# One more pair of gate panels by the seven-product scheme: 30 instead of 28 of 32, with token blocks made sooner and PSUM banks mirrored

## Chip, cores and metric

One core of one Trainium2 chip. The metric is the device time of one execution in microseconds (us). Engines are called by their names in the profile: PE (TensorE, matmuls), PEld (its weight loads), DVE (VectorE), ACT (ScalarE), POOL (GpSimd), SP (SyncE, which here only starts transfers). Two times of this kernel that differ by under 0.2% (2.2 us) can't be told from no change.

## What is computed

Two layers, one behind the other, on 512 tokens of width 1024. The change lies in the end of the second:

```
h = rms_norm_2(x, norm_g)
proj = h @ w_in                      # its last 4 x 1024 columns are the gates
...
ys = jnp.stack([y_a, y_b, y_c, y_d], axis=0)           # four branches, 512 wide each
branch_d = jnp.einsum('nbsw,nwd->bsnd', ys, w_branch)
g = jax.nn.sigmoid(gates.reshape(bsz, s, N_BRANCH, d))
merged = jnp.sum(g * branch_d, axis=2)
return x + merged @ w_out
```

followed by a last RMS norm. All products are to fp32 accuracy: every operand is split in two fp32r parts, hi and lo, and each product of two operands is three matmuls (hi hi, hi lo, lo hi).

## The kernel before, in words

The program is written out by hand for each engine, with semaphores between them. The work is a list of **units**, `USED`; PE, ACT and DVE each walk the same list in order, and each engine's own queue is strictly in order. A unit is mostly one weight strip of 128 x 1024. For unit number k:

- SP fetches strips into a ring of five raw buffers, in the order of the list; a buffer is free once the strip in it has been split (`raw_done`, `lo_made`).
- ACT, in its turn for unit k, first makes the hi part of the strip of unit k+3 (`split_hi`, L665, one copy). DVE, in its turn for unit k, first forms a sum or difference of weights for unit k+4 where there is one (`combine`), then makes the lo part of unit k+3 (`split_lo`, L1201, one subtraction). Then both do what unit k's own results want: ACT a sigmoid or copies out of PSUM, DVE products and sums. ACT waits for PE's end of unit k ahead of those (not in units `sa` and `br`).
- PE multiplies the strip with the transposed tokens hT, 8 tiles of 128 x 512, hi and lo.

The gates are 32 panels `ga` of 128 output columns, the branches' output products are 16 units `br`; pair p = 2 panels `ga 2p`, `ga 2p+1` and one unit `br p`. A panel done plainly is 8 tiles x 3 = 24 matmuls of 512 columns (`panel`, `product`, L1896 to L1898). Pairs 2 to 15 are done instead by a seven-product scheme (as Strassen's, in Winograd's form): the two panels, 1024 inputs and 512 tokens are cut in halves, and seven products of quarters are made, each 4 x 3 = 12 matmuls of 256 columns (`quarters`, L1904 to L1908). They are spread over the units `sa` (2 products), `sb` (2), `br` (1, between the two halves of the branch product; the branch product itself is 24 matmuls of 512), `sc` (1) and `sd` (1), in the function `strassen`. Pairs take turns in the PSUM banks side and acc (`banks_of`).

The chain within one pair: after the first product of `sa` (12 matmuls) ACT copies it out of bank 0 to gate_a (semaphore `part_kept`); the second half of unit `sb` adds to that bank and therefore waits for this copy. The copy stands in ACT's turn for unit `sa`, behind `split_hi` of the unit three further on. The product in the middle of `br` waits likewise for a second copy, and for the lo weights of `sc`.

The scheme needs **token blocks** that are sums and differences of quarters of hT: T1, T2, T4 (with hi and lo) and T3, which is written over the quarter (0,1) of hT once no plain panel reads that any more. `make_tokens` (DVE) makes each: three chained 128 x 1024 operations for the full value (`difference`, L1227 to L1229; T3 and T4), one subtraction for the lo part; ACT makes the hi part with a copy. T1 and T2 are made long before, in units `dq` and `dk`. The order around the change, before it (one unit each, plain letters for plain units):

```
dz3 | ga0 | ga1 | br0 | ga2 | ga3 | br1 | sa2 | sb2 | br2 | sc2 | sd2 | sa3 ...
DVE: dz3 -; ga0 four y_d tiles; ga1 T3 full; ga2 T4 full; ga3 T4 lo; br1 T3 lo
ACT: ga0 hi of four y_d tiles; ga3 T4 hi, then T3 hi
```

In DVE's turn for ga0 the last branch, y_d, is ended: four times a product (L1430), a copy by ACT (L918), a subtraction (L1434), in lockstep. For the first pair by the scheme, `sb` wants T1 and T2, the middle product of `br` wants T3 lo, and `sc` wants T4 lo.

Of the kernel before, what the change touches and what calls it, by code (L numbers as in the profile page):

```python
# [6 lines left out]
P = 128  # L7
S = 512
# [42 lines left out]

FIRST_PAIR, LAST_PAIR = 2, 2 * KT - 1
USED = []
for u in ORDER:
    if u[0] == "br" and u[1] >= FIRST_PAIR:
# [180 lines left out]
def program(nc, dram, out):  # L238
    f32, f32r, bf16, i32 = mybir.dt.float32, mybir.dt.float32r, mybir.dt.bfloat16, mybir.dt.int32
    ALU, ACT, AX = mybir.AluOpType, mybir.ActivationFunctionType, mybir.AxisListType  # L240
    with ExitStack() as ctx:
# [159 lines left out]
        t_rest = {n: at(f"t{n}_rest", r, [P, 4, HALF]) for n, r in ((1, R_B), (4, M + 16384))}  # L401
        t_full = {n: at(f"t{n}_full", r + 4096, [P, 4, HALF]) for n, r in ((1, R_B), (2, R_B + 8192), (4, M + 16384))}
        s12 = at("s12", M + 24576, [P, 2, 4 * P])
        t3_part = at("t3_part", M + 24576, [P, 4, HALF])
        t3_full = at("t3_full", M + 28672, [P, 4, HALF])
        gate_a = at("gate_a", R_0, [P, S])
        gate_b = at("gate_b", M + 28672, [P, HALF])
        x2_kept = nc.dram_tensor("x2_kept", (S, D), f32, kind="Internal").ap()
# [98 lines left out]
        def strip_of(k):  # L507

            kind, j = USED[k]
            if kind == "sa":  # L510
                return raw_of(("ga", 2 * j))
            if kind == "sb":
                return s12[:, :, :].rearrange("p a c -> p (a c)")
            if kind == "sc":
                return raw_of(("ga", 2 * j + 1))
            if kind == "sd":
                return raw_of(("ga", 2 * j))[:, 512:1024]
            return raw[:, UNIT[kind, j] % RING, 0:WIDTH.get(kind, U)]

        def banks_of(p):  # L520

            return side if p % 2 == 0 else acc

        def ada_tile(j):
            return ada_raw[j % ADA_RING // 4][:, j % 4, :]
# [116 lines left out]
        def _(act):  # L642
# [238 lines left out]
            for k, (kind, j) in enumerate(USED):  # L881
# [168 lines left out]
                if (kind, j) in (("dq", 2), ("dq", 3)):  # L1050
                    n = j - 1
                    act.wait_ge(t_step, T_STEP[n, "full"])
                    nc.scalar.activation(t_hi[n][:, :, :], t_full[n][:, :, :], ACT.Copy).then_inc(t_hi_made, 1)
                if (kind, j) == ("ga", 3):
                    act.wait_ge(t_step, T_STEP[4, "full"])
                    nc.scalar.activation(t_hi[4][:, :, :], t_full[4][:, :, :], ACT.Copy).then_inc(t_hi_made, 1)
                    act.wait_ge(t_step, T_STEP[3, "full"])
                    nc.scalar.activation(quarter(hT_hi, 0, 1), t3_full[:, :, :], ACT.Copy).then_inc(t_hi_made, 1)
# [50 lines left out]
        def _(dve):  # L1109
# [94 lines left out]
            def combine(k):  # L1204

                kind, j = USED[k] if k < len(USED) else (None, 0)
                if kind not in ("sb", "sc", "sd"):
                    return
                a, b, n = raw_of(("ga", 2 * j)), raw_of(("ga", 2 * j + 1)), j - FIRST_PAIR + 1
                if kind == "sb":  # L1210
                    for u in (("ga", 2 * j), ("ga", 2 * j + 1)):
                        dve.wait_ge(raw_in[UNIT[u] % RING], 16 * (UNIT[u] // RING + 1))
                    then(nc.vector.tensor_tensor(out=s12[:, 0, :], in0=b[:, 0:512], in1=b[:, 512:1024], op=ALU.add))
                    nc.vector.tensor_tensor(out=s12[:, 1, :], in0=s12[:, 0, :], in1=a[:, 0:512], op=ALU.subtract)\
                        .then_inc(combined, 1)
                if kind == "sc":
                    nc.vector.tensor_tensor(out=b[:, 0:512], in0=a[:, 0:512], in1=b[:, 0:512], op=ALU.subtract)\
                        .then_inc(combined, 1)
                if kind == "sd":
                    dve.wait_ge(combined, 3 * (n - 1) + 1)  # L1220
                    dve.wait_ge(lo_made, STEP["sa", j] + 1)
                    nc.vector.tensor_tensor(out=a[:, 512:1024], in0=a[:, 512:1024], in1=s12[:, 1, :], op=ALU.subtract)\
                        .then_inc(combined, 1)

            def difference(dst, part, hi, lo, hi_less, lo_less):
# [5 lines left out]
            def make_tokens(kind, j):  # L1231

                hi = {(r, c): quarter(hT_hi, r, c).bitcast(f32) for r in (0, 1) for c in (0, 1)}
                lo = {(r, c): quarter(hT_lo, r, c).bitcast(f32) for r in (0, 1) for c in (0, 1)}
                full, rest = {n: t[:, :, :] for n, t in t_full.items()}, {n: t[:, :, :] for n, t in t_rest.items()}
                if (kind, j) == ("dq", 1):
                    dve.wait_ge(x2_saved, 16)
                    difference(full[1], rest[1], hi[0, 1], lo[0, 1], hi[0, 0], lo[0, 0])
                if (kind, j) == ("dq", 2):
                    dve.wait_ge(t_step, T_STEP[1, "full"])  # L1240
                    then(nc.vector.tensor_tensor(out=full[2], in0=hi[1, 1], in1=full[1], op=ALU.subtract))
                    nc.vector.tensor_tensor(out=full[2], in0=full[2], in1=lo[1, 1], op=ALU.add).then_inc(t_step, 1)
                if (kind, j) in (("dq", 3), ("dk", 0)):
                    n = 1 if kind == "dq" else 2
                    dve.wait_ge(t_step, T_STEP[2, "full"])
                    dve.wait_ge(t_hi_made, n)
                    nc.vector.tensor_tensor(out=t_lo[n][:, :, :], in0=full[n], in1=t_hi[n][:, :, :].bitcast(f32),
                                            op=ALU.subtract).then_inc(t_step, 1)
                if (kind, j) == ("ga", 1):
                    difference(t3_full[:, :, :], t3_part[:, :, :], hi[1, 1], lo[1, 1], hi[0, 1], lo[0, 1])  # L1250
                if (kind, j) == ("ga", 2):
                    dve.wait_ge(t_step, T_STEP[2, "lo"])
                    difference(full[4], rest[4], hi[1, 0], lo[1, 0],
                               t_hi[2][:, :, :].bitcast(f32), t_lo[2][:, :, :].bitcast(f32))
                if (kind, j) == ("ga", 3):
                    dve.wait_ge(t_step, T_STEP[4, "full"])
                    dve.wait_ge(t_hi_made, 3)
                    nc.vector.tensor_tensor(out=t_lo[4][:, :, :], in0=full[4], in1=t_hi[4][:, :, :].bitcast(f32),
                                            op=ALU.subtract).then_inc(t_step, 1)
                if (kind, j) == ("br", 1):  # L1260
                    dve.wait_ge(t_step, T_STEP[3, "full"])
                    dve.wait_ge(t_hi_made, 4)
                    nc.vector.tensor_tensor(out=quarter(hT_lo, 0, 1), in0=t3_full[:, :, :],
                                            in1=quarter(hT_hi, 0, 1).bitcast(f32), op=ALU.subtract).then_inc(t_step, 1)

            def gate_pair(kind, j):
# [12 lines left out]
                if kind == "sd":  # L1279
# [5 lines left out]
                    for o in (1, 0):  # L1285
                        dve.wait_ge(unit_used, STEP["br", j] + 1)
                        dve.wait_ge(sig_made, 3 * p + 3 - o)
                        first = j % 2 == 0 and o == 1
                        nc.vector.tensor_tensor(out=total if first else merged_part[:, :], in0=(acc if o == 0 else side)[3][:, :],
                                                in1=sig[:, o, :], op=ALU.mult).then_inc(gated, 1)  # L1290
                        dve.wait_ge(gated, 2 * p + 2 - o)
                        if not first:
# [285 lines left out]
            for k, (kind, j) in enumerate(USED):  # L1578
# [271 lines left out]
                if (kind, j) == ("w2", 3):  # L1850
                    for t in range(TT):
                        if t == 0:
                            dve.wait_ge(x2_here, 32)
                        wait_tile(dve, (kind, j), t)
                        nc.vector.tensor_tensor(out=x2[t][:, 0:S], in0=side[t][:, :], in1=x2[t][:, 0:S],
                                                op=ALU.add).then_inc(freed["dve"], 1)
                if (kind, j) == ("w2", 4):

# [8 lines left out]
                if (kind, j) == ("w2", 7):  # L1867
# [5 lines left out]

                    for t in range(TT):
                        wait_tile(dve, (kind, j), t)
                        nc.vector.tensor_tensor(out=x2[t][:, S:D], in0=acc[t][:, :], in1=x2[t][:, S:D],
                                                op=ALU.add).then_inc(freed["dve"], 1)
                        if t:
                            finish_right(t - 1)
# [3 lines left out]
        def _(pe):  # L1883
# [28 lines left out]
            def strassen(k, kind, j):  # L1912
# [4 lines left out]
                if kind == "sa":  # L1917
# [3 lines left out]
                        pe.wait_ge(bank2_read, len(BANK2))  # L1921
                        pe.wait_ge(bank3_read, 2 * TT)
                    elif p == 1:
                        wait_freed(pe, RESULT["br", 1] + 1)
                    else:
                        pe.wait_ge(sig_made, 3 * (p - 1))
                    quarters(ps[0], w, 0, h[0, 0]).then_inc(part_made, 1)
# [8 lines left out]
                if kind == "br":  # L1936
                    hi, lo = weights(k)
                    if p == 0:
                        wait_freed(pe, RESULT["br", 1] + 1)
                    else:  # L1940
                        pe.wait_ge(gated, 2 * p)
                    for o in range(2):
                        if o == 1:
# [3 lines left out]
                                pe.wait_ge(t_step, T_STEP[3, "lo"])  # L1947
                            quarters(ps[0], w, 0, h[0, 1], first=False).then_inc(part_made, 1)
                        name = "abcd"[2 * (j % 2) + o]
                        for kt in range(4):  # L1950
                            cols = slice((4 * o + kt) * P, (4 * o + kt + 1) * P)
                            ins = product((acc if o == 0 else side)[3][:, :], (hi[:, cols], lo[:, cols]),
                                          (y_hi[name][:, kt, :], y_lo[name][:, kt, :]), kt == 0, kt == 3)
                    ins.then_inc(unit_used, 1)
                if kind == "sc":
# [24 lines left out]
            def token_units(k, kind, j, source, width, x_ready=None, tile_done=None, early=None):  # L1980

                per, count = TOKEN_UNITS[kind], TOGETHER.get((kind, j), 1)
                for t in range(TT):
# [4 lines left out]
                    for i in range(count - 1, -1, -1):  # L1988
                        hi, lo = weights(k - i, t == 0)
                        first, last = (j - i) % per == 0, (j - i) % per == per - 1  # L1990
                        if kind == "w2":
# [4 lines left out]
                            if (j - i, t) == (4, 0):  # L1996
                                pe.wait_ge(sig_made, 3 * (LAST_PAIR - FIRST_PAIR + 1))
                                pe.wait_ge(gated, 2 * (LAST_PAIR - FIRST_PAIR + 1))
                            ps = (side if j - i < per else acc)[t]
                        else:  # L2000
                            ps = bank(r) if first else acc[r % 4]
                        for a in range(2):
# [486 lines left out]
```

## Time and profile before

| | |
|---|---|
| median of 3 runs | 1106.76 us (1106.72 to 1107.06) |
| the profiled execution | 1106.82 us |
| its span, first to last instruction | 1104.9 us |
| PE busy | 1096.4 us, 99% of the span |
| PEld / DVE / ACT / POOL busy | 84% / 68% / 47% / 2% |
| mean granted clock of PE | 0.998 |
| DMA | 121.09 MB, mean 110 GB/s |

The execution is 1.9 us longer than its span. Busy time of PE counts a matmul to the end of its pipeline, so matmuls that follow one another overlap in it; what a matmul costs is the distance from its start to the next one's start.

### The profile page before, as it was taken

To read this page: it belongs to the slowest core of one execution; us is meant where nothing else is said; L and a number is where in the kernel's file an instruction comes from. 1 tells how busy PE (TensorE), PEld (TensorE's weight loads), DVE (VectorE), ACT (ScalarE), POOL (GpSimd) and SP (SyncE) were. 2 spreads that over 40 slices of the span, in tenths; PEclk is the share of its full clock that TensorE was granted. 3 is DMA by queue.
4 is the path that set the end of the run, shared out by engine and by line. 5 is a ranking of instruction groups with operands and counts; after the bars stand their busy time and mean duration, and the time that the engine had idled before them with its cause. 6 is when DMAs were issued, how large, how long until landed. Compare 5 with 4: busy or idle time off the path is not lost.

```text
span 1104.9 us, 17994 instructions
## 1 busy us (share of the span) xinstructions
PE 1096.4 (99%) x7298; PEld 928.7 (84%) x7298; DVE 748.9 (68%) x1202; ACT 517.5 (47%) x870; POOL 17.8 (2%) x40
## 2 busy tenths in 40 slices
PE   9999999999999999999999999999999999999997
PEld 8888888888888888878888887887789999999986
DVE  6876876954676247458789887447568777667853
ACT  7662354324675235544453535336544444444543
POOL 1000000000001001000000000000000000000000
PEclk9999999999999999999999999999999999999999
DMA  9543324422214422622222232231121322333241
GB/s 371 221 152 125 120 74 133 125 98 78 77 58 144 161 90 104 200 66 86 79 77 96 77 96 77 63 109 58 58 77 58 115 100 73 115 114 115 83 185 77
DMA packets 33618, 121.09 MB, mean 110 GB/s; under 512 B 3824, under 2 KB 3824, under 8 KB 33536
## 3 DMA queue, kind: packets, MB, share of 16 engines
q1 hardware_dynamic: 30672, 109.88, 29.2%
q0 software_dynamic: 2720, 10.03, 2.6%
q8 instruction: 58, 0.95, 0.3%
q14 instruction: 24, 0.20, 0.1%
q10 hardware_dynamic: 144, 0.03, 0.0%
HBM read 115.74 MB, written 4.19 MB: 109 GB/s over the span
## 4 chain that ended last, share of the span: by engine, by line
PE 98%; DMA 1%; ACT 0%; SPq 0%; DVE 0%; issue 0%
PE acc L1896 22%; PE acc L1898 22%; PE acc L1897 22%; PE acc L1908 2%; PE side L1908 2%; PE acc L1906 2%; PE side L1906 2%; PE acc L1904 2%; PE side L1904 2%; PE side L1896 2%; PE side L1897 2%; PE side L1898 2%; PE acc L2271 2%; PE side L2051 2%; PE side L2271 1%; PE side L2123 1%
## 5 line engine op out<-in xcount | busy, mean ns | idle before, releaser
L1201 DVE TENSOR_TENSOR w_lo<-raw,w_hi 128x1024 fp32r<-128x1024 f32 (+2 forms) x194 | 225.7, 1165 | 148.9 <-ACT w_hi L665 146.1
L1896 PE MATMUL acc<-hT_hi,w_hi 128*128 128x512 f32 x648 | 258.6, 399 | 0.0
L1898 PE MATMUL acc<-hT_hi,w_lo 128*128 128x512 f32 x648 | 252.8, 390 | 0.0
L1897 PE MATMUL acc<-hT_lo,w_hi 128*128 128x512 f32 x648 | 252.4, 389 | 0.0
L665 ACT ACTIVATE w_hi<-raw 128x1024 fp32r<-128x1024 f32 (+2 forms) x194 | 195.4, 1008 | 109.8 <-PE acc L1898 82.4
L1896 PEld LDWEIGHTS acc<-hT_hi,w_hi 128*128 128x128 f32 x648 | 121.8, 188 | 27.1 <-issue 2.4
L1898 PEld LDWEIGHTS acc<-hT_hi,w_lo 128*128 128x128 f32 x648 | 121.6, 188 | 26.0
L1897 PEld LDWEIGHTS acc<-hT_lo,w_hi 128*128 128x128 f32 x648 | 121.9, 188 | 23.6
L1896 PE MATMUL acc<-w_hi,hT_hi 128*128 128x512 f32 (+1 forms) x152 | 59.9, 394 | 0.0
L1898 PE MATMUL acc<-w_hi,hT_lo 128*128 128x512 f32 (+1 forms) x152 | 58.8, 387 | 0.0
L1897 PE MATMUL acc<-w_lo,hT_hi 128*128 128x512 f32 (+1 forms) x152 | 58.7, 386 | 0.0
L1201 DVE TENSOR_TENSOR w_lo<-s,w_hi 128x1024 fp32r<-128x1024 f32 x14 | 17.1, 1225 | 39.7 <-ACT w_hi L665 39.7
L944 ACT ACTIVATE silu_e<-acc 128x512 f32<-128x512 f32 x32 | 18.9, 592 | 53.6 <-PE acc L1898 53.6
L1896 PEld LDWEIGHTS acc<-w_hi,hT_hi 128*128 128x128 f32 x152 | 28.5, 188 | 6.1 <-issue 0.8
L1898 PEld LDWEIGHTS acc<-w_hi,hT_lo 128*128 128x128 f32 x152 | 28.5, 188 | 5.6
L1897 PEld LDWEIGHTS acc<-w_lo,hT_hi 128*128 128x128 f32 x152 | 28.6, 188 | 5.2
L1908 PE MATMUL side<-hT_hi,w_lo 128*128 128x256 f32 x112 | 31.7, 283 | 0.0
L1908 PE MATMUL acc<-hT_hi,w_lo 128*128 128x256 f32 x112 | 31.7, 283 | 0.0
L1906 PE MATMUL side<-hT_lo,w_hi 128*128 128x256 f32 x112 | 31.7, 283 | 0.0
L1906 PE MATMUL acc<-hT_lo,w_hi 128*128 128x256 f32 x112 | 31.7, 283 | 0.0
L1904 PE MATMUL acc<-hT_hi,w_hi 128*128 128x256 f32 x112 | 31.7, 283 | 0.0
L1904 PE MATMUL side<-hT_hi,w_hi 128*128 128x256 f32 x112 | 31.7, 283 | 0.0
(482 smaller groups left out, 2249.0 us busy)
## 6 DMA issues: line engine op xcount, KB each, us to landing
raw<-in_ga SPq DMA_DIRECT2D x32, 512.0 KB, 4.8
ada_raw<-in_ada SPq DMA_DIRECT2D x16, 512.0 KB, 11.5
raw<-in_wo SPq DMA_DIRECT2D x16, 512.0 KB, 3.5
raw<-in_br SPq DMA_DIRECT2D x16, 512.0 KB, 3.5
raw<-in_q SPq DMA_DIRECT2D x8, 512.0 KB, 3.5
raw<-in_u SPq DMA_DIRECT2D x8, 512.0 KB, 3.9
raw<-in_gp SPq DMA_DIRECT2D x8, 512.0 KB, 4.8
raw<-in_ada_w SPq DMA_DIRECT2D x8, 512.0 KB, 3.5
```

Of the source, the lines that this page charges most:

```text
L665: nc.scalar.activation(split_at(k)[0][:, 0:WIDTH.get(kind, U)], strip_of(k), ACT.Copy).then_inc(hi_made, 1)
L944: nc.scalar.activation(gate_e(gates), acc[RESULT[kind, j] % 4][:, :], ACT.Exp, scale=-1.0)\
L1201: nc.vector.tensor_tensor(out=lo[:, 0:width], in0=strip_of(k), in1=hi[:, 0:width].bitcast(f32), op=ALU.subtract).then_inc(lo_made, 1)
L1896: nc.tensor.matmul(ps, w[0], x[0], start=first, stop=False)
L1897: nc.tensor.matmul(ps, w[0], x[1], start=False, stop=False)
L1898: return nc.tensor.matmul(ps, w[1], x[0], start=False, stop=last)
L1904: nc.tensor.matmul(out_, w[0][:, cols], x[0][:, kt, :], start=first and kt == 0, stop=False, skip_group_check=not first)
L1906: nc.tensor.matmul(out_, w[0][:, cols], x[1][:, kt, :], start=False, stop=False, skip_group_check=not first)
L1908: ins = nc.tensor.matmul(out_, w[1][:, cols], x[0][:, kt, :], start=False, stop=kt == 3, skip_group_check=not first)
L2051: ins = nc.tensor.matmul(ps[p0:p0 + B, n0:n0 + width], k[:, tok], right, start=True, stop=True)
L2123: ins = nc.tensor.transpose(side[2][:, b * P:(b + 1) * P], probs[:, s % 2, b * P:(b + 1) * P], ident[:, :])
L2271: return nc.tensor.matmul((acc + side)[h][:, :], w[:, h * P:(h + 1) * P], x[:, j, :], start=start and j == 0, stop=stop and j == KT - 1)
```

## The change

Pair 1 (panels ga2 and ga3) goes by the seven-product scheme too. `FIRST_PAIR` becomes 1, and the list reads `dz3 | ga0 | ga1 | br0 | sa1 | sb1 | br1 | sc1 | sd1 | sa2 ...`. DVE makes T3 full in its turn for dz3 (was ga1), T4 full for ga1 (was ga2), T4 lo for br0 (was ga3), T3 lo for sa1 (was br1). ACT makes T4 hi and T3 hi in its turn for br0 (was ga3). The sum of weights of the first pair has a place of its own (`s12_first`), as has T3. Banks: the first pair still begins in side, so all later pairs, and the two halves of the last product, change sides.

```diff
-FIRST_PAIR, LAST_PAIR = 2, 2 * KT - 1
+FIRST_PAIR, LAST_PAIR = 1, 2 * KT - 1
...
+        s12_first = at("s12_first", M + 4096, [P, 2, 4 * P])
-        t3_part = at("t3_part", M + 24576, [P, 4, HALF])
-        t3_full = at("t3_full", M + 28672, [P, 4, HALF])
+        t3_part = at("t3_part", M + 8192, [P, 4, HALF])
+        t3_full = at("t3_full", M + 12288, [P, 4, HALF])
...
-        def banks_of(p):
+        def s12_of(j):
+            return s12_first if j == FIRST_PAIR else s12
+        def banks_of(j):
-            return side if p % 2 == 0 else acc
+            return side if (j - FIRST_PAIR) % 2 == 0 else acc
...
-                if (kind, j) == ("ga", 3):
+                if (kind, j) == ("br", 0):
+                    act.wait_ge(unit_used, STEP["ga", 1] + 1)
                     act.wait_ge(t_step, T_STEP[4, "full"])
                     nc.scalar.activation(t_hi[4][:, :, :], t_full[4][:, :, :], ACT.Copy).then_inc(t_hi_made, 1)
                     act.wait_ge(t_step, T_STEP[3, "full"])
...
+                if (kind, j) == ("dz", 3):
+                    difference(t3_full[:, :, :], t3_part[:, :, :], hi[1, 1], lo[1, 1], hi[0, 1], lo[0, 1])
                 if (kind, j) == ("ga", 1):
-                    difference(t3_full[:, :, :], t3_part[:, :, :], hi[1, 1], lo[1, 1], hi[0, 1], lo[0, 1])
-                if (kind, j) == ("ga", 2):
                     dve.wait_ge(t_step, T_STEP[2, "lo"])
                     difference(full[4], rest[4], hi[1, 0], lo[1, 0],
                                t_hi[2][:, :, :].bitcast(f32), t_lo[2][:, :, :].bitcast(f32))
-                if (kind, j) == ("ga", 3):
+                if (kind, j) == ("br", 0):
...
-                if (kind, j) == ("br", 1):
+                if (kind, j) == ("sa", 1):
                     dve.wait_ge(t_step, T_STEP[3, "full"])
...
-                        wait_freed(pe, RESULT["br", 1] + 1)
+                        wait_freed(pe, RESULT["br", 0] + 1)
...
+                        if p == 0:
+                            pe.wait_ge(y_made, 1 + FINAL.index((name, 3)))
                         for kt in range(4):
                             cols = slice((4 * o + kt) * P, (4 * o + kt + 1) * P)
-                            ins = product((acc if o == 0 else side)[3][:, :], (hi[:, cols], lo[:, cols]),
+                            ins = product((side if o == 0 else acc)[3][:, :], (hi[:, cols], lo[:, cols]),
...
-                            ps = (side if j - i < per else acc)[t]
+                            ps = (acc if j - i < per else side)[t]
```

The reads of these banks by DVE (branch products times gates, and the two sums with the residual at the end) change sides with them.

## Rows read from the trace of the kernel before

**Rows 1.** The page's part 1 and the chain of waits (part 4), share of the span.

```profile
PE 1096.4 (99%) x7298; PEld 928.7 (84%) x7298; DVE 748.9 (68%) x1202; ACT 517.5 (47%) x870; POOL 17.8 (2%) x40
...
PE 98%; DMA 1%; ACT 0%; SPq 0%; DVE 0%; issue 0%
```

**Rows 2.** PE's timeline, 821 to 853 us: start, length, line, out<-in.

```profile
821.04 0.39 PE L1896 MATMUL acc<-hT_hi,w_hi 128*128 128x512 f32 x1
...
837.36 0.28 PE L1904 MATMUL side<-hT_hi,w_hi 128*128 128x256 f32 x1
...
843.11 0.40 PE L1896 MATMUL acc<-ya_hi,w_hi 128*128 128x512 f32 x1
...
845.86 0.28 PE L1904 MATMUL side<-hT_hi,w_hi 128*128 128x256 f32 x1
...
847.29 0.40 PE L1896 MATMUL side<-yb_hi,w_hi 128*128 128x512 f32 x1
...
850.04 0.28 PE L1904 MATMUL side<-t_hi,w_hi 128*128 128x256 f32 x1
...
852.91 0.28 PE L1904 MATMUL acc<-hT_hi,w_hi 128*128 128x256 f32 x1
```

**Rows 3.** DVE's timeline, 803 to 843 us; in brackets idle time before, releaser.

```profile
803.75 0.43 DVE L1372 TENSOR_SCALAR silu_e<-silu_e 128x512 f32<-128x512 f32 x1 [2.65 <-ACT silu_e L944]
806.48 1.22 DVE L1201 TENSOR_TENSOR w_lo<-raw,w_hi 128x1024 fp32r<-128x1024 f32 x1 [2.31 <-ACT w_hi L665]
...
808.27 0.68 DVE L1430 TENSOR_TENSOR y_tmp<-z_d,yd_raw 128x512 f32<-128x512 f32 x1
...
819.07 1.23 DVE L1201 TENSOR_TENSOR w_lo<-raw,w_hi 128x1024 fp32r<-128x1024 f32 x1 [2.10 <-ACT w_hi L665]
820.22 1.22 DVE L1227 TENSOR_TENSOR t_full<-hT_hi 128x1024 f32<-128x1024 f32 x1
...
822.73 1.23 DVE L1229 TENSOR_TENSOR t_full<-t_full,t_part 128x1024 f32<-128x1024 f32 x1
823.87 1.22 DVE L1201 TENSOR_TENSOR w_lo<-raw,w_hi 128x1024 fp32r<-128x1024 f32 x1
825.01 0.68 DVE L1831 TENSOR_TENSOR m_full<-acc,sig 128x512 f32<-128x512 f32 x1
...
827.17 0.69 DVE L1213 TENSOR_TENSOR s<-raw 128x512 f32<-128x512 f32 x1
...
828.51 1.22 DVE L1201 TENSOR_TENSOR w_lo<-raw,w_hi 128x1024 fp32r<-128x1024 f32 x1
...
841.48 0.68 DVE L1222 TENSOR_TENSOR raw<-raw,s 128x512 f32<-128x512 f32 x1
842.08 1.22 DVE L1201 TENSOR_TENSOR w_lo<-raw,w_hi 128x1024 fp32r<-128x1024 f32 x1
```

**Rows 4.** ACT's timeline, 833 to 839 us.

```profile
833.42 1.06 ACT L1056 ACTIVATE t_hi<-t_full 128x1024 fp32r<-128x1024 f32 x1 [0.70 <-DVE t_full L1229]
834.38 1.04 ACT L1058 ACTIVATE hT_hi<-t_full 128x1024 fp32r<-128x1024 f32 x1
835.33 1.04 ACT L665 ACTIVATE w_hi<-raw 128x1024 fp32r<-128x1024 f32 x1
...
838.99 0.38 ACT L1064 ACTIVATE gate_a<-side 128x256 f32<-128x256 f32 x1
```

**Rows 5.** SP's timeline and the transfers of 780 to 860 us, median landing time last.

```profile
807.73 0.33 SPq L564 DMA_DIRECT2D raw<-in_br  x1
...
raw<-in_br SPq DMA_DIRECT2D x3, 512.0 KB, 3.7
```

**Rows 6.** The last matmul, then stretches: length, busy PE, ..., granted clock (PEclk), DMA.

```profile
1098.52 0.39 PE L1898 MATMUL acc<-w_hi,m_lo 128*128 128x512 f32 x1
...
1101.00:1102.00 1.00, 0.00 (x0) 0.00 (x0) 0.75 (x1) 0.72 (x1) 0.00 (x0) 0.76 0.80 328
1102.00:1103.00 1.00, 0.00 (x0) 0.00 (x0) 0.00 (x0) 0.00 (x0) 0.00 (x0) 0.50 0.87 344
```

More of the change, by code:

```diff
@@ L512, in strip_of @@
             if kind == "sb":
-                return s12[:, :, :].rearrange("p a c -> p (a c)")
+                return s12_of(j)[:, :, :].rearrange("p a c -> p (a c)")
             if kind == "sc":
@@ L1208, in combine @@
                     return
+                part = s12_of(j)
                 a, b, n = raw_of(("ga", 2 * j)), raw_of(("ga", 2 * j + 1)), j - FIRST_PAIR + 1
@@ L1212, in combine @@
                         dve.wait_ge(raw_in[UNIT[u] % RING], 16 * (UNIT[u] // RING + 1))
-                    then(nc.vector.tensor_tensor(out=s12[:, 0, :], in0=b[:, 0:512], in1=b[:, 512:1024], op=ALU.add))
-                    nc.vector.tensor_tensor(out=s12[:, 1, :], in0=s12[:, 0, :], in1=a[:, 0:512], op=ALU.subtract)\
+                    then(nc.vector.tensor_tensor(out=part[:, 0, :], in0=b[:, 0:512], in1=b[:, 512:1024], op=ALU.add))
+                    nc.vector.tensor_tensor(out=part[:, 1, :], in0=part[:, 0, :], in1=a[:, 0:512], op=ALU.subtract)\
                         .then_inc(combined, 1)
@@ L1221, in combine @@
                     dve.wait_ge(lo_made, STEP["sa", j] + 1)
-                    nc.vector.tensor_tensor(out=a[:, 512:1024], in0=a[:, 512:1024], in1=s12[:, 1, :], op=ALU.subtract)\
+                    nc.vector.tensor_tensor(out=a[:, 512:1024], in0=a[:, 512:1024], in1=part[:, 1, :], op=ALU.subtract)\
                         .then_inc(combined, 1)
@@ L1288, in gate_pair @@
                         first = j % 2 == 0 and o == 1
-                        nc.vector.tensor_tensor(out=total if first else merged_part[:, :], in0=(acc if o == 0 else side)[3][:, :],
+                        nc.vector.tensor_tensor(out=total if first else merged_part[:, :], in0=(side if o == 0 else acc)[3][:, :],
                                                 in1=sig[:, o, :], op=ALU.mult).then_inc(gated, 1)
@@ L1854, in _ @@
                         wait_tile(dve, (kind, j), t)
-                        nc.vector.tensor_tensor(out=x2[t][:, 0:S], in0=side[t][:, :], in1=x2[t][:, 0:S],
+                        nc.vector.tensor_tensor(out=x2[t][:, 0:S], in0=acc[t][:, :], in1=x2[t][:, 0:S],
                                                 op=ALU.add).then_inc(freed["dve"], 1)
@@ L1875, in _ @@
                         wait_tile(dve, (kind, j), t)
-                        nc.vector.tensor_tensor(out=x2[t][:, S:D], in0=acc[t][:, :], in1=x2[t][:, S:D],
+                        nc.vector.tensor_tensor(out=x2[t][:, S:D], in0=side[t][:, :], in1=x2[t][:, S:D],
                                                 op=ALU.add).then_inc(freed["dve"], 1)
@@ L1938, in strassen @@
                     if p == 0:
-                        wait_freed(pe, RESULT["br", 1] + 1)
+                        wait_freed(pe, RESULT["br", 0] + 1)
                     else:
```

## Prediction

> **What bounds the kernel now.** First the page: PE is busy 99% of the span, and 98% of the chain of waits is PE's [rows 1]. So a saving on PE counts in full, and so does every wait put on PE; the other engines have room on the whole (DVE 68%), which says nothing of a single stretch. So I read the timelines of PE, DVE and ACT around the change, 795 to 855 us. On PE, units follow one another without a gap, also from plain panels into the first pair by the scheme [rows 2]. On DVE there is idle time before 819 us (2.3 us before the subtraction at 806.48, 2.1 us before that at 819.07), and from there on none: operation follows operation until past 842 [rows 3]. The token blocks are made there. That stretch decides.
>
> **PE's work.** Plainly, pair 1 takes 821.04 to 837.36 = 16.32 us (72 matmuls of 512 columns, 0.2267 us each). By the scheme, pair 2 takes 837.36 to 852.91 = 15.55 us [rows 2]. 48 matmuls of 512 become 84 of 256, 0.1198 us each (48 of them from 837.36 to 843.11). The columns fall by an eighth, the time by less, since half the columns take more than half of 0.2267. **Gain: 0.77 us.**
> By the Trainium skill (TensorE: Matmul & The Clock Gate, "Back-to-back issue gap") a matmul costs its columns at 2.4 GHz and 2.5 ns; that would make 48 x 215.8 - 84 x 109.2 ns = 1.2 us, an estimate; the trace has 227 and 120 ns for this mix with weight loads, so the trace's 0.77 us stands.
> Even without any new wait the gain is thus 0.07%, a third of what can be told from no change (0.2%, 2.2 us).
>
> **DVE in the new order.** Start to start [rows 3]: a full token block 3.65 us (820.22 to 823.87); a 1024 subtraction 1.15 (819.07 to 820.22); both weight sums of `sb` 1.34 (827.17 to 828.51); one weight difference 0.60 (841.48 to 842.08); gating br0 2.16 (825.01 to 827.17).
> - dz3: T3 can start behind the bound of the gate at 803.75, so at 804.1, and ends DVE's work there at 807.75. Before, DVE was idle until 806.48.
> - ga0: weight sums of `sb1`, new here, 1.34: 809.1. Then w_lo and gate as before (1.79, 806.48 to 808.27): 810.9 instead of 808.27. **DVE is 2.6 us late.** The four y_d tiles are in lockstep with ACT, and ACT's first sigmoid and next weight copy come behind them, so this isn't won back: the subtraction of 819.07 comes at 821.7. It is now `sb1`'s strip, done 822.9; PE wants it at 823.9: in time, with 1 us to spare.
> - ga1: T4 full runs where T3 full ran, 2.6 us later: 822.8, last of three operations at 825.3, ended **826.6**.
> - br0: from 826.5 (1.15 after T4's last start) difference for `sc1` 0.6, w_lo of `br1` 1.15 (ended 828.3), gating 2.16, T4 lo 1.15 (ended 831.7): 831.6.
> - sa1: difference for `sd1` 0.6, w_lo of `sc1` 1.15 (ended 833.4), then T3 lo, 1.22 long, 833.35 to **834.6**.
>
> **ACT in the new order** [rows 4]. In its turn for br0 it now waits for T4 full, and queued behind that wait are T4 hi, T3 hi, the hi weights of `sc1`, and, in the turn for sa1, the copy to gate_a for which PE waits. Before, T3 hi ended at 835.4 and the copy came at 838.99, when PE's first product was there: the wait for T4 was over before `sa2` began, since br1 lay between. Now: T4 hi 826.6, T3 hi 827.6, w_hi 828.5 (0.95 each), copy 829.5 to **829.85**.
>
> **PE in the new order** [rows 2]. br0 still ends at 821.04. `sa1` 24 x 0.12 = 2.9: 823.9. First half of `sb1` 1.44: 825.35. Then the wait for the copy, to 829.9: **4.5 us of idle PE, the first new wait.** Second half of `sb1` to 831.35; first half of the branch product 2.75 (843.11 to 845.86): 834.1; w_lo of `sc1` is ready since 833.4, T3 lo isn't: to 834.6, **0.5 us, the second.** What is left of the pair is 852.91 - 845.86 = 7.05 us: `sa2` starts at 841.65 instead of 837.36. **+4.3 us** = 4.5 + 0.5 - 0.77. T4 lo (831.7) and y_d (819.6) are in time. From `sa2` on the order and the relative times are those of today's pairs, which have no wait, and PE never has slack in which to win it back.
>
> **Beside it, at nothing.** SP: the raw buffer of ga2 is free only after `sd1` (w_lo about 835.4) instead of at 807.7, and `br2`'s strip and those of the next panels queue behind that. It lands some 3.7 us later [rows 5], 839.1; ACT wants it after `sc1` ends, about 840.3. If that cover were gone, each us of lateness would be one on PE; bounds 0 and +1, I take 0. The weight sums of `sb1` want both strips of pair 1 in ga0; they follow dz2 and dz3 in the ring and are there tens of us before. POOL's transfers wait for the same named units. Mirrored banks and halves move no work and no time. New waits of PE for branches c and d repeat semaphores long reached. DVE's four operations that gate br1 are four in the new way too; the three short sums of products that come with a pair (gate_a, gate_b) lie behind T3 lo, where today's pairs leave DVE idle time.
>
> **PE's clock.** After the last matmul ended (1098.9), the granted clock read 1.00, then 0.76 over 1101 to 1102 and 0.50 after [rows 6]: it fell to 1.2 GHz at about 1101.5, after 2.6 us of idle PE. The new gap is 4.4 us, so it can fall here. No row has a matmul at the lower level; at it, a spacing doubles. Bounds: 0 if it doesn't fall; if it stays low for all of the 4.2 us of work up to the wait for T3 lo, +4.2, less the 0.5 that this wait gives back: +3.7. I take a short fall, as likely as none: low for about as long as it took to fall, 2.6 us, costs 1.3 - 0.5 = 0.8, half of which is **+0.4**.
> The Trainium skill (same page, "Why this matters for your kernels") warns that a pause of this kind between bursts puts the clock back to half; by it the clock falls for certain, and the rival below gains.
>
> **Sum**: 1106.82 (the profiled execution: span 1104.9 and 1.9 around it; 0.06 over the median of 1106.76) - 0.77 + 4.55 + 0.5 + 0.4 = **1111.5 us**.
>
> **Rivals.**
> - The clock falls and stays low up to the next wait. For: [rows 6]. Against: at the start of that work PE is fully busy again. Time 1111.1 + 1.2 to 3.7 = 1112.3 to 1114.8. Chance 0.20.
> - Not slower: T3 in dz3 costs DVE nothing. For: 2.3 us were idle before the subtraction at 806.48 and 2.1 us at 819.07. Were DVE not late at all, T4 full would end at 824.0, the copy at 827.3: a wait of 1.9, then 0.5 for T3 lo, less 0.77: 1108.5, within 0.2%. It decides once DVE is less than 0.5 us late at 819. Against: T3 and the weight sums are 5.0 us and only 2.3 of idle time precede, while the 2.1 us at 819 are a wait for ACT, which is shifted as well. Chance 0.06.
> - No new wait on PE at all, if the copy to gate_a doesn't stand behind T4's wait in ACT's queue as I read the list: 1106.05, gain alone. The order in the code speaks against it. Chance 0.05, of which 0.01 for a gain of over 0.2% by something not seen here.
> - The ring: `br2`'s strip and its followers are late on top of the two waits. For: it is fetched 28 us later than now; three transfers start together. Against: today's pairs live with the same distance. 1 us more, 1112.5. Chance 0.06.
> - The forecast, 1110.6 to 1112.3: chance 0.63.
>
> **Numbers.** Faster by over 0.2% 0.02; within 0.2% (1104.6 to 1109.0) 0.11; slower 0.87. The range leaves out the two cases below 1109 and the top of the clock's: 1109.6 to 1113.6.
>
> **What would show it.** PE's timeline: no gap between the first two units of the scheme, then a gap of about 4.5 us in the middle of `sb1` put down to ACT's gate_a, a shorter one in the middle of `br1` put down to DVE's hT_lo; PE idle by some 5 us more, the number of matmuls up by 36. ACT: T4 hi at about 826.6, with 4 to 5 us of idle time before it, released by DVE's T4 full. DVE: the first y_d product at 810.9. Granted clock around 829 to 834: 1.00, or 0.50 in part. Wrong would be: `sb1` without a gap (the ACT order is misread), DVE on time at 819 (T3 was free), a later gap before `br2` (the ring).

## The result, and the profile after

The changed kernel took 1112.11 us in the median of 5 runs (1111.85 to 1113.21), the kernel before 1106.76 us: **0.52% slower** (ratio 1.0052, 95% interval 1.0041 to 1.0062), 5.35 us. Five more runs, beside another series of 21 runs of the kernel before, gave 1113.05 against 1106.97 us (1.0053, 1.0041 to 1.0066). The profiled execution shown here is the longest of the first five, 1113.21 us, 6.4 us over that of the kernel before.

The page of the changed kernel (span; part 1; the chain of part 4):

```profile
span 1111.3 us, 18091 instructions
...
PE 1098.6 (99%) x7334; PEld 932.3 (84%) x7334; DVE 754.3 (68%) x1211; ACT 520.0 (47%) x876; POOL 17.8 (2%) x40
...
PE 96%; DVE 1%; ACT 1%; DMA 1%; issue 0%; SPq 0%; DVEq 0%; ACTq 0%
```

PE has 36 matmuls more, and its share of the chain fell from 98% [rows 1] to 96%; DVE and ACT, at 0% before, now have 1% each. PE's timeline (start, length, line, out<-in, in brackets idle time before and its releaser; answers to [rows 2]):

```profile
820.83 0.28 PE L1910 MATMUL side<-hT_hi,w_hi 128*128 128x256 f32 x1
...
825.02 0.28 PE L1914 MATMUL side<-t_hi,w_lo 128*128 128x256 f32 x1
829.64 0.58 PE L1910 MATMUL side<-t_hi,w_hi 128*128 128x256 f32 x1 [4.34 <-ACT gate_a L1069]
830.02 0.41 PE L1912 MATMUL side<-t_lo,w_hi 128*128 128x256 f32 x1
...
832.37 0.63 PE L1902 MATMUL side<-yc_hi,w_hi 128*128 128x512 f32 x1
832.80 0.63 PE L1903 MATMUL side<-yc_lo,w_hi 128*128 128x512 f32 x1
...
836.02 0.39 PE L1902 MATMUL side<-yc_hi,w_hi 128*128 128x512 f32 x1
836.25 0.39 PE L1903 MATMUL side<-yc_lo,w_hi 128*128 128x512 f32 x1
...
836.72 0.28 PE L1910 MATMUL side<-hT_hi,w_hi 128*128 128x256 f32 x1
...
843.76 0.28 PE L1910 MATMUL acc<-hT_hi,w_hi 128*128 128x256 f32 x1
```

br0 ends and `sa1` begins at 820.83, 0.21 us earlier than in the execution of before. The first half of `sb1` issues its last matmul at 825.02; then PE is idle for 4.34 us and is released by ACT's copy to gate_a. What follows is to be read by its spacing, the distance from one matmul's start to the next one's: 829.64 to 832.37 is 12 matmuls in 2.73 us, 0.21 us each once the first is through (0.12 before), and 832.37 to 832.80 is 0.43 us for a matmul of 512 columns (0.227 before). Not until 836.02 is the spacing 0.23 again. `sa2` begins at 843.76: 22.93 us after `sa1`, where the pair has 15.55 us of work. By spacing, the 7.38 us between them are the wait (825.14 to 829.64, 4.50) and the slow stretch behind it (829.64 to 836.72 is 7.08 us for work that takes 4.19, 1.44 + 2.75, in the rows of before).

DVE's timeline (answers to [rows 3]: T3's first operation, first y_d product, w_lo of `sb1`, T4's last operation, T3 lo):

```profile
803.88 1.22 DVE L1233 TENSOR_TENSOR t_full<-hT_hi 128x1024 f32<-128x1024 f32 x1
...
810.60 0.68 DVE L1436 TENSOR_TENSOR y_tmp<-z_d,yd_raw 128x512 f32<-128x512 f32 x1
...
821.40 1.23 DVE L1206 TENSOR_TENSOR w_lo<-s_first,w_hi 128x1024 fp32r<-128x1024 f32 x1 [2.10 <-ACT w_hi L669]
...
825.05 1.23 DVE L1235 TENSOR_TENSOR t_full<-t_full,t_rest 128x1024 f32<-128x1024 f32 x1
...
832.98 1.22 DVE L1269 TENSOR_TENSOR hT_lo<-t_full,hT_hi 128x1024 fp32r<-128x1024 f32 x1
```

ACT's timeline (answers to [rows 4]: T4 hi, T3 hi, w_hi of `sc1`, the copy to gate_a):

```profile
826.37 1.06 ACT L1061 ACTIVATE t_hi<-t_full 128x1024 fp32r<-128x1024 f32 x1 [3.57 <-DVE t_full L1235]
827.34 1.04 ACT L1063 ACTIVATE hT_hi<-t_full 128x1024 fp32r<-128x1024 f32 x1
828.28 1.04 ACT L669 ACTIVATE w_hi<-raw 128x1024 fp32r<-128x1024 f32 x1
829.23 0.36 ACT L1069 ACTIVATE gate_a<-side 128x256 f32<-128x256 f32 x1
```

The y_d tiles start 2.33 us later than at 808.27 [rows 3] (2.54 if the 0.21 us between the executions are counted), T4 full ends at 826.28, and behind it ACT makes four copies back to back. The last of them, the copy of 0.36 us to gate_a, is what PE wants; it ends at 829.59.

PE's granted clock in stretches of one us (length, busy PE, PEld, DVE, ACT, POOL, clock, DMA share, GB/s; answers to [rows 6]):

```profile
828.00:829.00 1.00, 0.00 (x0) 0.00 (x0) 0.96 (x3) 1.00 (x2) 0.00 (x0) 0.98 0.00 0
829.00:830.00 1.00, 0.35 (x1) 0.36 (x2) 0.97 (x2) 0.59 (x2) 0.00 (x0) 0.50 0.00 0
...
834.00:835.00 1.00, 1.00 (x4) 0.73 (x3) 1.00 (x3) 0.00 (x0) 0.00 (x0) 0.50 0.00 0
835.00:836.00 1.00, 1.00 (x4) 0.79 (x3) 0.97 (x3) 0.00 (x0) 0.00 (x0) 0.61 0.02 8
836.00:837.00 1.00, 1.00 (x7) 0.84 (x6) 1.00 (x2) 0.00 (x0) 0.00 (x0) 1.00 0.56 184
```

The clock fell at 828.96 (0.98 over the us from 828), 3.7 us after PE's last matmul had ended, and stayed at its lower level of 1.2 GHz for 6.8 us, to 835.8 (a reading of 0.61 over one us means 0.78 us at the lower level). The strip of `br2` is fetched where it was forecast, and PE never waits for it:

```profile
835.16 0.33 SPq L568 DMA_DIRECT2D raw<-in_br  x1
```

### The profile page after: what moved, and what is told of

It is laid out like the page before. It is cut to its first block, busy times and chain, and to the rows that moved or that the text cites. A ratio compares the mean times of both kernels' runs of the same rounds, so it can differ in the third digit from the quotient of the medians.

```text
span 1111.3 us, 18091 instructions
## 1 busy us (share of the span) xinstructions
PE 1098.6 (99%) x7334; PEld 932.3 (84%) x7334; DVE 754.3 (68%) x1211; ACT 520.0 (47%) x876; POOL 17.8 (2%) x40
## 3 DMA queue, kind: packets, MB, share of 16 engines
HBM read 115.74 MB, written 4.19 MB: 108 GB/s over the span
## 4 chain that ended last, share of the span: by engine, by line
PE 96%; DVE 1%; ACT 1%; DMA 1%; issue 0%; SPq 0%; DVEq 0%; ACTq 0%
PE acc L1902 21%; PE acc L1904 21%; PE acc L1903 21%; PE side L1910 2%; PE side L1914 2%; PE side L1912 2%; PE side L1902 2%; PE side L1903 2%; PE side L1904 2%; PE acc L1914 2%; PE acc L1912 2%; PE acc L1910 2%; PE acc L2279 2%; PE side L2059 2%; PE side L2279 1%; PE side L2131 1%
## 5 line engine op out<-in xcount | busy, mean ns | idle before, releaser
L1902 PE MATMUL acc<-hT_hi,w_hi 128*128 128x512 f32 x632 | 252.4, 399 | 0.0
L1904 PE MATMUL acc<-hT_hi,w_lo 128*128 128x512 f32 x632 | 246.5, 390 | 0.0
L1903 PE MATMUL acc<-hT_lo,w_hi 128*128 128x512 f32 x632 | 246.1, 389 | 0.0
L1902 PEld LDWEIGHTS acc<-hT_hi,w_hi 128*128 128x128 f32 x632 | 118.8, 188 | 26.5 <-issue 2.4
L1904 PEld LDWEIGHTS acc<-hT_hi,w_lo 128*128 128x128 f32 x632 | 118.6, 188 | 25.4
L1903 PEld LDWEIGHTS acc<-hT_lo,w_hi 128*128 128x128 f32 x632 | 118.9, 188 | 23.0
L1914 PE MATMUL side<-hT_hi,w_lo 128*128 128x256 f32 x128 | 36.2, 283 | 0.0
L1912 PE MATMUL side<-hT_lo,w_hi 128*128 128x256 f32 x128 | 36.2, 283 | 0.0
L1910 PE MATMUL side<-hT_hi,w_hi 128*128 128x256 f32 x128 | 36.2, 283 | 0.0
L1910 PE MATMUL side<-t_hi,w_hi 128*128 128x256 f32 x96 | 27.8, 290 | 4.3 <-ACT gate_a L1069 4.3
```

The source lines that it names most:

```text
L1902: nc.tensor.matmul(ps, w[0], x[0], start=first, stop=False)
L1903: nc.tensor.matmul(ps, w[0], x[1], start=False, stop=False)
L1904: return nc.tensor.matmul(ps, w[1], x[0], start=False, stop=last)
L1910: nc.tensor.matmul(out_, w[0][:, cols], x[0][:, kt, :], start=first and kt == 0, stop=False, skip_group_check=not first)
L1912: nc.tensor.matmul(out_, w[0][:, cols], x[1][:, kt, :], start=False, stop=False, skip_group_check=not first)
L1914: ins = nc.tensor.matmul(out_, w[1][:, cols], x[0][:, kt, :], start=False, stop=kt == 3, skip_group_check=not first)
```

## Experiments

All runs of a group share their runs of the kernel before: 1106.78 us (1106.59 to 1107.05) for the first four, 1106.97 us (1106.81 to 1107.53) for the last three, another chip with 0.19 us more. That 0.19 us is taken off where the two groups are compared. Most differences between these kernels are under the 0.2% that can't be told from no change by one comparison; what is said of them rests on series of runs that don't overlap, and on the waits in the traces.

### Is ACT's order at fault, or DVE's chain?

```diff
-                if (kind, j) == ("br", 0):
-                    act.wait_ge(unit_used, STEP["ga", 1] + 1)
-                    act.wait_ge(t_step, T_STEP[4, "full"])
-                    nc.scalar.activation(t_hi[4][:, :, :], t_full[4][:, :, :], ACT.Copy).then_inc(t_hi_made, 1)
...
                     nc.scalar.activation(gate_a[:, 0:HALF], banks_of(j)[0][:, 0:HALF], ACT.Copy).then_inc(part_kept, 1)
+                    if p == 0:
+                        act.wait_ge(t_step, T_STEP[4, "full"])
+                        nc.scalar.activation(t_hi[4][:, :, :], t_full[4][:, :, :], ACT.Copy).then_inc(t_hi_made, 1)
...
```

> ACT's copies T4 hi and T3 hi moved from its turn for br0 to its turn for sa1, behind the copy to gate_a. Theory (DVE's chain sets the time, ACT's queue only passes it on): the hi weights of sc1 still stand ahead of the copy and want DVE's weight difference, ended 826.9; so the copy ends about 828.3 and the first gap of PE shrinks from 4.5 to about 3.1 us, but T3 lo comes at 834.2 as before and PE waits there for 1.7 us more if its clock is high. Time 1110.9 with the clock at 1.00, about 1112.1 if it falls as in the changed kernel: within 0.3 us of 1111.1 or of 1112.1, no gain to speak of. Rival (ACT's order alone is at fault): the gap's 1.4 us are gained in full, 1110.7 or less beside 1112.1, and no second gap.

Measured: 1111.14 us (1111.10 to 1111.26), 1.0039 (1.0027 to 1.0052). PE's two gaps, from its timeline:

```profile
828.47 0.39 PE L1909 MATMUL side<-t_hi,w_hi 128*128 128x256 f32 x1 [3.00 <-ACT gate_a L1063]
...
834.52 0.36 PE L1909 MATMUL side<-hT_hi,w_hi 128*128 128x256 f32 x1 [1.60 <-DVE hT_lo L1268]
```

The first gap shrank by 1.34 us to 3.00, and a second of 1.60 us opened, for T3 lo. The clock reads 1.00 all through the units of pair 1 in this execution, and by spacing the two waits are 3.16 and 1.76 us: together 4.9, as in the forecast for the changed kernel (4.5 + 0.5). (One of the five runs had a mean clock of 0.997 and was no longer than the others; a second wait of this length can take a slow stretch up, which is argued, not shown. So the times of this kernel don't tell whether the clock fell.) The theory holds: a better order on ACT only moves the wait to the next thing that DVE's chain makes late. Beside the changed kernel it is 1 us faster all the same, and the next run tells what that us was.

### What is the clock's part?

```diff
+                    if p == 0:
+                        wait_freed(pe, RESULT["ga", 1])
+                        for _ in range(36):
+                            nc.tensor.matmul(acc[RESULT["ga", 1] % 4][:, 0:HALF], w[0][:, 0:P],
+                                             t[1][0][:, 0, :], start=True, stop=True)
                     pe.wait_ge(part_kept, 3 * p + 1)
```

> 36 more matmuls of 256 columns (4.3 us at 0.12 us each) put on PE in the middle of sb1, ahead of its wait for the copy to gate_a, into an accumulator bank that is free then; their result is not used. Theory (the low clock after the gap is worth the difference between the wait alone and what was measured): granted clock 1.00 all through 825 to 840 us, spacings of 0.12 and 0.227 us behind the gap, T3 lo awaited for 0.5 us, time 1111.0 to 1111.2 in every run, 1 us under the changed kernel's median and with a spread of 0.2 us instead of 1.4. Rival (the clock has no part in it, the spread comes from elsewhere): 1112.1 and the same spread; or slower, if these matmuls disturb DVE's reads.

Measured: 1111.17 us (1110.98 to 1111.41). Clock in stretches of 2 us:

```profile
828.00:830.00 2.00, 1.97 (x17) 1.77 (x16) 1.93 (x4) 1.79 (x3) 0.00 (x0) 1.00 0.00 0
830.00:832.00 2.00, 2.00 (x15) 1.91 (x16) 1.97 (x3) 0.00 (x0) 0.00 (x0) 1.00 0.03 8
...
834.00:836.00 2.00, 1.75 (x14) 1.50 (x13) 1.97 (x5) 0.01 (x1) 0.00 (x0) 1.00 0.01 4
```

PE does 4.3 us of work for nothing, and the kernel is 0.94 us faster by the medians. The clock stays at 1.00, T3 lo is awaited (0.25 us of idle PE, 0.40 by spacing), and the time is the forecast's without its clock term, 1111.1. The spread is 0.4 us instead of 1.4, twice the 0.2 expected, with two of the five runs (1111.33 and 1111.41) above the 1111.2 that was expected at the most. So the rest of what the changed kernel lost is the clock.

The changed kernel once more, in the second group:

> The changed kernel as it is, for more runs of it beside the others. Theory (a gap of 4.3 us, and the clock falls behind it in every run, at a moment that differs): all runs above the 1111.2 of the kernel with the filled gap, from 1111.8 to 1113.3, the more the lower the mean clock. Rival (it falls in some runs only): some runs at 1111.0 to 1111.3.

Measured: 1113.05, 1113.35, 1112.32, 1113.43 and 1112.29 us, with mean clocks of 0.997, 0.995, 0.997, 0.996 and 0.998. Less 0.19 they lie between 1112.1 and 1113.2; the shortest of the ten runs of this kernel, 1111.85, is longer than the longest with the filled gap, 1111.41. That the clock fell in all ten is seen in the two traces and concluded for the others from their times. In the profiled execution (1113.05 us) the gap is again 4.34 us, and the clock fell later, about when PE began again, and was low for 3.6 us only:

```profile
830.00:831.00 1.00, 0.32 (x2) 0.33 (x3) 0.97 (x2) 0.62 (x2) 0.00 (x0) 1.00 0.00 0
831.00:832.00 1.00, 1.00 (x7) 1.00 (x6) 0.97 (x2) 0.00 (x0) 0.00 (x0) 0.51 0.00 0
...
834.00:835.00 1.00, 1.00 (x5) 0.81 (x4) 1.00 (x2) 0.84 (x1) 0.00 (x0) 0.79 0.00 0
835.00:836.00 1.00, 1.00 (x6) 0.83 (x5) 1.00 (x3) 0.00 (x0) 0.00 (x0) 1.00 0.00 0
```

How long the clock is low thus differs from run to run (3.6 and 6.8 us), and so does its cost: here the work from 830.68 to 836.49 took 5.81 us instead of 4.19, +1.6. This execution also waited 1.5 us for ACT in its first 20 us, instead of 0.4, so its time doesn't follow from the clock alone.

### Is DVE's lateness the cause?

T3 full one unit sooner, where DVE has idle time:

```diff
-                if (kind, j) == ("dz", 3):
+                if (kind, j) == ("dz", 2):
                     difference(t3_full[:, :, :], t3_part[:, :, :], hi[1, 1], lo[1, 1], hi[0, 1], lo[0, 1])
```

> T3 full made one unit sooner still, in DVE's turn for dz2 instead of dz3, where DVE has 3.3 us of idle time. Theory (the 2.6 us by which DVE is late at 819 come from T3, and go straight into the wait): weight sums of sb1 fit into the idle time before 806.5, first y_d product at 808.1 instead of 810.6, T4 full ends 824.0 instead of 826.3, first gap of PE 2.0 us instead of 4.5, second 0.5; clock stays at 1.00 as the gap is shorter than the 2.6 us of the end of the kernel: 1106.05 + 1.9 + 0.5 = 1108.4 (1108.2 to 1108.7). If the clock falls all the same: up to 1110.8. Rival (the wait is set by ACT's own work, not by DVE's lateness): no less than 1111.

Measured: 1109.64 us in the median of 11 runs (1108.51 to 1109.86), ratio 1.0022 (1.0013 to 1.0031). DVE (weight sum, first y_d product, T4's last operation), then PE's two gaps, in the profiled execution of 1108.54 us:

```profile
804.06 0.69 DVE L1219 TENSOR_TENSOR s_first<-raw 128x512 f32<-128x512 f32 x1
...
808.24 0.68 DVE L1436 TENSOR_TENSOR y_tmp<-z_d,yd_raw 128x512 f32<-128x512 f32 x1
...
822.70 1.22 DVE L1235 TENSOR_TENSOR t_full<-t_full,t_rest 128x1024 f32<-128x1024 f32 x1
```

```profile
827.29 0.38 PE L1910 MATMUL side<-t_hi,w_hi 128*128 128x256 f32 x1 [1.81 <-ACT gate_a L1069]
...
831.98 0.35 PE L1910 MATMUL side<-hT_hi,w_hi 128*128 128x256 f32 x1 [0.26 <-DVE hT_lo L1269]
```

DVE is in time at 808.24, T4 full ends at 823.92, and the first gap is 1.81 us of idle PE, the second 0.26. This execution, 1108.54 us, is what was expected (1108.2 to 1108.7). But the median missed it: only five of the eleven runs are near it (1108.51 to 1108.89, mean clock 0.998 to 1.000); six are at 1109.64 to 1109.86 with 0.997. The expectation that the clock stays up behind so short a gap was wrong, if the next run is read rightly: the same kernel with 15 such matmuls in its first gap.

> The kernel with T3 in dz2 and 15 more matmuls of 256 columns (1.8 us) in PE's first gap, ahead of its wait. That kernel's eleven runs fell in two groups, five at 1108.5 to 1108.9 with a mean clock of 0.998 to 1.000, six at 1109.6 to 1109.9 with 0.997. Theory (the upper group is runs in which the clock fell after the gap of 1.8 us, the lower group is the wait alone): with the gap filled only the lower group is left, 1108.5 to 1108.8 in every run. Rival (two groups for another reason, as the second wait or the transfers): both groups again.

Measured: 1108.81 us (1108.74 to 1109.12, 11 runs; less 0.19: 1108.55 to 1108.93, at most 0.1 us over what was expected). The upper group is gone, though the second gap is still there (0.25 us). So behind a gap of 1.8 us the clock fell in six runs of eleven, at 1.1 us each, and behind 4.3 us in ten of ten. For the six this is concluded from the two groups, their mean clocks and this run; the profiled execution of that kernel is one of the five, and its clock stayed at 1.00 behind the gap. A longer gap doesn't always bring the fall: in the profiled execution of the first experiment the clock stayed at 1.00 behind 3.00 us.

### All of it moved, and the gain alone

T3 full goes to dz2, T4 full to dz3 (its part of the lo values first, as the memory for the full value is read by PE until then), T4 hi and lo to ga0, T3 hi and lo to ga1, with the weight difference of `sc1` ahead of T3 lo; that of `sd1` goes behind w_lo of `sc1`. ACT makes the first pair's two copies to gate_a ahead of its weight copies, and PE waits for br0's bank only before the second half of br1. The core of the diff:

```diff
+                if (kind, j) == ("dz", 3):
+                    dve.wait_ge(t_step, T_STEP[2, "lo"])
+                    dve.wait_ge(bank2_read, len(BANK2))
+                    then(nc.vector.tensor_tensor(out=rest[4], in0=lo[1, 0], in1=t_lo[2][:, :, :].bitcast(f32),
+                                                 op=ALU.subtract))
+                    dve.wait_ge(bank3_read, 2 * TT)
...
-                if (kind, j) == ("sa", 1):
+                if (kind, j) == ("ga", 1):
+                    combine(STEP["sc", 1])
                     dve.wait_ge(t_step, T_STEP[3, "full"])
...
+                if (kind, j) == ("sa", 1):
+                    act.wait_ge(part_made, 1)
+                    nc.scalar.activation(gate_a[:, 0:HALF], side[0][:, 0:HALF], ACT.Copy).then_inc(part_kept, 1)
+                if (kind, j) == ("sb", 1):
+                    act.wait_ge(unit_used, k + 1)
+                    nc.scalar.activation(gate_a[:, HALF:], side[0][:, 0:HALF], ACT.Copy).then_inc(part_kept, 1)
                 if (kind, j) not in (("wo", 14), ("wo", 15)):
                     for later_k in to_split(k):
                         split_hi(later_k)
...
-                    if p == 0:
-                        wait_freed(pe, RESULT["br", 0] + 1)
...
+                            if o == 1:
+                                wait_freed(pe, RESULT["br", 0] + 1)
```

> The work is put where each engine is idle: T3 full in dz2, T4 full in dz3, T4 hi ahead of the y_d copies in ga0, T4 lo behind them, T3 hi and T3 lo in ga1, the copies to gate_a of the first pair ahead of ACT's weight copy, the weight difference of sc1 a unit sooner and that of sd1 behind w_lo of sc1, PE's wait for br0's bank just before the product that needs it. Theory (PE's work is 0.77 us less, and all of the rest was waits): no gap of PE above 0.1 us between 820 and 845, clock 1.00, 1106.0 (1105.8 to 1106.3), 0.7 us under the kernel before, which its runs (spread 0.1 to 0.3 us) can show. Rival (the scheme on one more pair costs something beyond the waits, as DMA, banks or DVE's load): 1106.8 or more without a gap in that stretch.

Measured: 1106.05 us (1105.83 to 1106.22, 11 runs) against 1106.78 us (1106.59 to 1107.05, 21 runs): 0.73 us less, and no run of the one is as long as any of the other. The interval of the ratio, 0.9985 to 1.0002 about 0.9993, includes no change, and 0.73 us is under the 0.2% that one comparison can tell; the trace is what shows it. PE's timeline (`sa1`, `sa2`) and the only waits of PE in the whole kernel, both in its first 20 us:

```profile
820.81 0.28 PE L1925 MATMUL side<-hT_hi,w_hi 128*128 128x256 f32 x1
...
836.37 0.28 PE L1925 MATMUL acc<-hT_hi,w_hi 128*128 128x256 f32 x1
```

```profile
PE acc L2270 <- POOL ones L589: 1.7, 1, 1.7
PE acc L2246 <- ACT turn_x L683: 0.7, 3, 0.4
```

The pair takes 15.56 us without a gap, the same as every pair by the scheme before, and 0.76 less than the 16.32 of the plain pair. The whole loss of the change was waits and the clock behind them; the scheme on one more pair costs nothing beyond.

DVE is no less late than in the changed kernel where the y_d tiles begin (T4's last operation, first y_d product):

```profile
806.63 1.23 DVE L1271 TENSOR_TENSOR t_full<-t_full,t_rest 128x1024 f32<-128x1024 f32 x1
...
810.84 0.68 DVE L1448 TENSOR_TENSOR y_tmp<-z_d,yd_raw 128x512 f32<-128x512 f32 x1
```

810.84 stands against 810.60 there and 808.27 before. What helps is that T4 full is now made ahead of those tiles, and ended at 807.86 instead of 826.28: lateness of DVE as such costs PE nothing, only that of the blocks that something waits for.

Whether the order on ACT matters once DVE makes the blocks early (edit against the kernel with all moved):

```diff
-                if (kind, j) == ("sa", 1):
-                    act.wait_ge(part_made, 1)
-                    nc.scalar.activation(gate_a[:, 0:HALF], side[0][:, 0:HALF], ACT.Copy).then_inc(part_kept, 1)
...
-                if kind == "sa" and p:
+                if kind == "sa":
```

> The kernel with all moved, but the first pair's two copies to gate_a back in their usual place behind ACT's weight copies. Theory (once DVE is in time, ACT's order decides): the first copy starts 0.95 us later, 824.8 instead of 823.9, and PE waits some 0.2 us for it; the second stands behind the hi weights of sd1, which want a difference that DVE ends at 829.65, so it ends at 830.6 while PE wants it at 829.3: 1.3 us. Time 1106.05 + 1.5 = 1107.5 (1107.2 to 1107.9). Rival (DVE's earlier work alone was the cure): 1106.05 to 1106.2.

Measured: 1107.78 us (1107.61 to 1107.99, 11 runs), less 0.19: 1.54 us over the kernel with all moved. ACT (first copy, w_hi of `sd1`, second copy), and the start of the product in the middle of br1 on PE:

```profile
825.24 0.38 ACT L1069 ACTIVATE gate_a<-side 128x256 f32<-128x256 f32 x1
830.10 0.63 ACT L669 ACTIVATE w_hi<-raw 128x512 fp32r<-128x512 f32 x1 [4.48 <-DVE raw L1228]
830.63 0.36 ACT L1071 ACTIVATE gate_a<-side 128x256 f32<-128x256 f32 x1
```

```profile
831.10 0.36 PE L1919 MATMUL side<-hT_hi,w_hi 128*128 128x256 f32 x1 [0.98 <-issue]
```

The second copy stands behind the weights of `sd1`, for which ACT waited 4.48 us, and PE goes on 0.11 us after it ends (the profile puts the 0.98 us of idle time down to no releaser; by spacing PE is 1.14 us late). The first copy, at 825.24 instead of 823.88 (0.42 us of that is where `sa1` begins), costs PE 0.23 us. Both halves of the cure were needed in this order of DVE's work: the blocks sooner (1111.17 with the clock kept up, to 1107.59), and nothing in ACT's queue ahead of the copy that wants something of DVE (to 1106.05).

## Why the prediction was right, point by point

Forecast 1111.5 us in a range of 1109.6 to 1113.6; measured 1112.11. The waits and their causes were forecast as they came, and the sum without its clock term, 1111.1, is within 0.1 us of what was measured with the clock kept up (1111.17). The clock term was too small.

- **PE's gain, 0.77 us.** Shown by the kernel with all moved: 16.32 us became 15.56 in the trace, and the time fell by 0.73 us. The trace's spacings decided it. The 1.2 us worked out from the rule of the Trainium skill (TensorE: Matmul & The Clock Gate, "Back-to-back issue gap"), which that section gives for an isolated matmul, would have been too much.
- **DVE 2.6 us late.** First y_d product at 810.60, forecast 810.9 (in this execution everything lies 0.21 us earlier). The idle time before the subtraction of 821.40 is 2.1 us as before: it was a wait for ACT, which is shifted too, and could not be won back. T4 full ended at 826.28, forecast 826.6. ACT's idle time before T4 hi was 3.57 us, where 4 to 5 were named as a sign.
- **The first wait.** ACT's four copies at 826.37, 827.34, 828.28, 829.23, forecast 826.6, 827.6, 828.5, 829.5, each 0.2 to 0.3 later than found, most of it the 0.21 us of offset. PE stood from 825.14 to 829.64, 4.50 us by spacing, forecast 4.5.
- **The second wait, 0.5 us.** In the changed kernel's profiled execution it is not to be seen: at the lower clock PE reached that point at 836.72, 2.5 us after T3 lo was there (834.20). With the clock kept up it is there, as forecast (0.25 us of idle PE behind the end of the last matmul's pipeline; 0.40 by spacing, and the product behind it takes 0.07 more).
- **The clock, +0.4 us: the term that was mis-sized.** It was the half of a short fall of 2.6 us, taken to be as likely as none. Two traces show falls of 6.8 and 3.6 us, and no run was without its cost: the ten lie 0.7 to 2.1 us above the 1111.17 of the filled gap, 0.94 by the medians of the first group. In the profiled execution of 1113.21 us the slow stretch cost 2.89 us, of which T3 lo's wait gives 0.5 back, so +2.4; in that of 1113.05 us it was 1.62 less 0.5, +1.1, and waits for ACT in the first 20 us were 0.5 us longer than with the filled gap (1.5 against 1.0). Five of the ten runs (1112.86 to 1113.24, those of the second group less 0.19) lie in the range of the rival in which the clock stays low up to the next wait (1112.3 to 1114.8), the other five just below its foot. Forecast case and this rival differ by degree only, and the chance of 0.20 for the latter was too low; that the median fell on the forecast's side of 1112.3 is in part luck. The warning of the Trainium skill (TensorE: Matmul & The Clock Gate, "Why this matters for your kernels") of what the clock does after such a pause is borne out by the ten runs of the changed kernel. The gap of 1.8 us is shorter than those that it warns of, and behind it the clock fell in six runs of eleven all the same; there the measurement decides. The end of the kernel before, with 2.6 us up to the fall [rows 6], was a fair guide that a gap of 4.4 us is long enough, but not that a shorter one is safe.
- **T3 free of charge on DVE**: not so in dz3, as argued; moving it to dz2 made it so. The time worked out for that rival, 1108.5, came in five runs of eleven; the other six had the clock's cost on top (median 1109.64).
- **The ring** was covered: `br2`'s strip was asked for at 835.16 (forecast 835.4), and no wait of PE is put down to it.
- **The chances** don't quite add up: the forecast, the clock's rival and the ring's give 0.89 for slower, where 0.87 is stated, and a gain over 0.2% has 0.01 among the rivals and 0.02 in the numbers. Nothing hangs on it.

## What to carry to other kernels

In strictly ordered queues follow the instruction that the bounding engine waits for, and list what stands ahead of it on its own engine with what each of those waits for: here a 0.36 us copy was late by 4.5 us for a block it doesn't use. Work moved earlier is free only if it lands in idle time that is not itself a wait for something shifted by the move. A saving under 1 us on the bounding engine was undone here by the first gap that the change opened there, and a gap on PE can cost more than its length, by the clock behind it (0.7 to 2.1 us more in the ten runs of this kernel). What counts is not how late an engine runs but how late it makes what is waited for.

## What was not expected of the hardware

- After an idle stretch of PE of only 1.8 us, in the midst of hundreds of us of dense work, six of eleven runs were 1.1 us longer, and filling the stretch with matmuls took that away: the granted clock fell, as far as times and mean clocks tell (no trace of such a run was kept). Behind 3.00 us it stayed at 1.00 in one traced execution of another order.
- Behind 4.3 us it fell to 1.2 GHz in both traced executions, and by their times in all ten. It fell 3.7 us after PE's last matmul had ended in one and 4.7 us in the other, and was low for 6.8 and 3.6 us, so the same gap cost different times.
- 4.3 us of useless matmuls in a gap made a kernel 0.94 us faster, and took the spread of its runs from 1.4 to 0.4 us.
